# Second block's attention in groups, its scan woven with projections, and a new step order for both blocks' group pipelines

## What is computed

```python
def first_block(...):                       # two layers
    h = _rms(x, ln1[l]) * (1 + sc1) + sh1
    x = x + g1 * _mixing(h, ...)            # top-k attention, stick-breaking, sliding window
    h = _rms(x, ln2[l]) * (1 + sc2) + sh2
    x = x + g2 * _swiglu(h, ...)

def _hybrid_mixer(h, ...):                  # second block, two layers
    proj = h @ w_in
    a_q, a_k, a_v, b_cq, b_ckv, b_kr, c_z, c_xbc, c_dt = split(proj)
    y_a = _diff_attention(a_q, a_k, a_v, lam, subln_g, lambda_init)  # softmax(s1) - lam * softmax(s2), then norm per head
    y_b = _mla(b_cq, b_ckv, b_kr, ...)      # keys and values from a low-rank part
    y_c = _mamba2(c_z, c_xbc, c_dt, ...)    # convolution, decayed scan, gate, group norm
    return concat([y_a, y_b, y_c]) @ w_out

x = x + g_m * _rmsnorm(_hybrid_mixer(h, ...), norm_g[l, 1])
```

## Time and profile before

| | us |
|---|---|
| time, median of 3 runs (lowest, highest) | 3538.05 (3533.71, 3542.37) |
| profiled execution: time, span | 3541.45, 3539.7 |
| PE busy in the span | 3192.5 (90%) |
| DVE busy | 1755.1 (50%) |
| POOL, ACT busy | 832.0 (24%), 705.4 (20%) |
| mean granted clock of PE | 0.913 |

### The profile page before, as it was taken

The page is one execution under the profiler, slowest core; times in us unless marked ns, Lnnn a source line. Parts: engine busy times, 40 slices in busy tenths (PEclk is TensorE's granted clock), DMA queues, the critical chain, the costliest instruction groups (busy, mean ns, idle before and its releaser), DMA issues.

```text
span 3539.7 us, 33580 instructions
## 1 busy us (share of the span) xinstructions
PE 3192.5 (90%) x12312; PEld 2192.8 (62%) x12312; DVE 1755.1 (50%) x3758; ACT 705.4 (20%) x1539; POOL 832.0 (24%) x704
## 2 busy tenths in 40 slices
PE   6877989999987788999979998899997998899996
PEld 3334548888733454888864452488884444378886
DVE  1375337775327543777542265495833347152343
ACT  2233320000113332000012241220202133121110
POOL 0120113444312011344430000144340000124442
PEclk8987799999998788999999978899998978899998
DMA  4111313443211001344221100144420210112221
GB/s 194 57 39 72 143 60 113 173 179 110 90 48 48 24 1 60 130 156 183 106 76 67 71 1 0 72 172 161 179 103 28 76 48 1 48 48 95 77 91 48
DMA packets 38546, 304.89 MB, mean 86 GB/s; under 512 B 4192, under 2 KB 4320, under 8 KB 23920
## 3 DMA queue, kind: packets, MB, share of 16 engines
q1 hardware_dynamic: 38352, 302.68, 23.3%
q0 software_dynamic: 32, 0.07, 0.0%
HBM read 300.63 MB, written 2.10 MB: 86 GB/s over the span
## 4 chain that ended last, share of the span: by engine, by line
PE 78%; DVE 11%; issue 4%; ACT 3%; DMA 2%; POOL 1%; DVEq 0%; SPq 0%; POOLq 0%; ACTq 0%
PE bank L950 43%; PE bank L928 16%; PE bank L1039 4%; PE bank L1294 1%; DVE SPT L2265 1%; PE bank L1147 1%; PE bank L1089 1%; PE bank L1278 1%; PE bank L1076 1%; PE bank L1026 1%; DMA ring<-in_slabs 1%; DVE sel L1931 1%; PE bank L1285 1%; PE bank L1013 1%; DVE m L1930 1%
## 5 line engine op out<-in xcount | busy, mean ns | idle before, releaser
L855 POOL TENSOR_TENSOR SPT<-ring 128x512 f32<-128x512 f32 (+2 forms) x140 | 170.3, 1216 | 1863.3 <-DMA ring<-in_slabs 1244.6
L928 PE MATMUL bank<-hT,ring 128*128 128x512 f32 (+1 forms) x960 | 422.2, 599 | 14.6 <-ACT hT L1604 6.5
L950 PE MATMUL bank<-U,ring 128*128 128x256 f32 x1728 | 406.5, 380 | 0.0
L950 PEld LDWEIGHTS bank<-U,ring 128*128 128x128 f32 x1728 | 326.3, 190 | 43.3
L928 PEld LDWEIGHTS bank<-hT,ring 128*128 128x128 f32 (+1 forms) x960 | 181.3, 190 | 252.1 <-issue 246.1
L1750 DVE SCALAR_TENSOR_TENSOR nw<-sel,c,nw 128x256 f32<-128x256 f32 x504 | 321.8, 638 | 23.2 <-DMA sel<-in_mod_pieces 5.5
L950 PE MATMUL bank<-hT,ring 128*128 128x256 f32 x1216 | 299.8, 397 | 22.4 <-ACT hT L1604 8.6
L950 PE MATMUL bank<-U,SPT 128*128 128x256 f32 x1296 | 311.2, 379 | 0.1
L950 PE MATMUL bank<-hT,SPT 128*128 128x256 f32 x1216 | 287.3, 379 | 0.0
L950 PEld LDWEIGHTS bank<-hT,ring 128*128 128x128 f32 x1216 | 230.3, 195 | 70.9 <-issue 17.2
L950 PEld LDWEIGHTS bank<-U,SPT 128*128 128x128 f32 x1296 | 246.2, 190 | 33.9 <-POOL SPT L860 0.5
(11 more groups left out here) (293 smaller groups left out, 4164.6 us busy)
## 6 DMA issues: line engine op xcount, KB each, us to landing
ring<-in_slabs SPq DMA_DIRECT2D x88, 2048.0 KB, 8.0
sel<-in_mod_pieces SPq DMA_DIRECT2D x144, 512.0 KB, 3.8
ring<-in_slabs SPq DMA_DIRECT2D x8, 1536.0 KB, 7.1
ring<-in_slabs SPq DMA_DIRECT2D x8, 1280.0 KB, 6.0
ring<-in_slabs SPq DMA_DIRECT2D x4, 1664.0 KB, 7.0
ring<-in_slabs SPq DMA_DIRECT2D x2, 1808.0 KB, 7.3
cst<-in_consts SPq DMA_DIRECT2D x1, 2120.0 KB, 24.3
ring<-in_slabs SPq DMA_DIRECT2D x2, 1056.0 KB, 5.3
```

Of the source, the lines that this page charges most:

```text
L855: pool.tensor_tensor(e1, a21, a22, ALU.add).then_inc(*pool_order.up())
L928: mm = pe.matmul(dst, lhs(k), rhs(k), start=(k == 0), stop=(k == n - 1))
L950: mm = pe.matmul(into[j][:, c:c + HALF], lhs[:, k, :], rhs[:, k, :], start=(begin and k == 0), stop=(end and k == kp - 1))
```

## The change

**Slots (both blocks).** A slot is now two chunks, an early one and a late one. Early: `on` of group j-3, then `sc` of group j. Late: `ot` of j-4 (one slot later than before), `pv` of j-2, `tp` of j-1. ACT copies the output of `pv` (and of `bpv`) from its bank as soon as it is there and squares the copy; DVE scales the copy.

**First block.** `pss` stands behind the second part of the next tile instead of behind its fourth.

**Second block.** Attention runs in groups too (`GROUPS2`, 6 of kind `m` with 4 or 2 heads, 12 of kind `d` with 2 heads or 1), `m` first. The division is left to the end (`on`); for `d` a new step `cb` combines both maps after the exponents, and the norm is taken per group from the copy, as in the first block. The order of a layer is: tiles 6 to 9, 4, 5 and the values; a weave of the other projections with the whole scan (called weave 1 here); a weave of tiles 14 to 17 with gate and norm of the scan and the `m` slots (weave 2); a weave of `wo 0` (half of the output projection, over the scan's outputs, 4 k-steps a tile) with the `d` slots (weave 3); then `wo 1`, which DVE adds to the first half. POOL adds up the squares of the output, and one matmul is left of `ys`. The same slabs' contents come in another order and cut; their sum is the same.

```diff
 def group_slots(groups):
-    for j in range(len(groups) + 3):
-        slot = []
+    for j in range(len(groups) + 4):
+        early, late = [], []
+        if 0 <= j - 3 < len(groups):
+            early.append(("on", groups[j - 3]))
         if j < len(groups):
-            slot.append(("sc", groups[j]))
+            early.append(("sc", groups[j]))
+        if 0 <= j - 4 < len(groups):
+            late.append(("ot", groups[j - 4]))
+        if 0 <= j - 2 < len(groups):
+            late.append(("pv", groups[j - 2]))
         if 0 <= j - 1 < len(groups):
-            slot.append(("tp", groups[j - 1]))
-        if 0 <= j - 3 < len(groups):
-            slot.append(("on", groups[j - 3]))
-        if 0 <= j - 2 < len(groups):
-            slot.append(("pv", groups[j - 2]))
-        if 0 <= j - 3 < len(groups):
-            slot.append(("ot", groups[j - 3]))
-        out.append(slot)
-    return [[st] for slot in out for st in slot]
+            late.append(("tp", groups[j - 1]))
+        out += [early, late]
+    return out
...
+        sums = [("pss", TILES1[m - 1])] if 0 <= m - 1 < 16 and TILES1[m - 1] in NORMED else []
+        rope = [("rope", TILES1[m - 2])] if 0 <= m - 2 < 16 and TILES1[m - 2] in ROPED else []
...
-        return [("pj", n, 0), ("pj", n, 1), ("pj", n, 2), ("proj", n)]
+        return [[("pj", n, 0)], [("pj", n, 1)] + sums, [("pj", n, 2)], [("proj", n)] + rope]
...
-UNITS2 = [("d", h, i) for i in range(QT) for h in range(4)] + [("m", h, i) for i in range(QT) for h in range(4)]
+GROUPS2 = [("m", 0, 4, 0), ("m", 0, 4, 1), ("m", 0, 2, 2), ("m", 2, 2, 2), ("m", 0, 2, 3), ("m", 2, 2, 3)]
+NM2 = len(GROUPS2)
+GROUPS2 += [("d", h, 2, i) for i in (0, 1) for h in range(2)] + [("d", h, 1, i) for i in (2, 3) for h in range(4)]
...
+        if 0 <= j - 3 < len(groups):
+            early.append(("on", groups[j - 3]))
+        if 0 <= j - 1 < len(groups) and GROUPS2[groups[j - 1]][0] == "d":
+            early.append(("cb", groups[j - 1]))
+        if j < len(groups):
+            early.append(("sc", groups[j]))
...
+    dense = [c for n in range(4) for c in tile2(n)]
+    dense[8] += [("cqss",)]
+    dense += [[("kvss",), ("kr",)]]
+    dense += [c for n in range(10, 14) for c in tile2(n)]
+    dense += [[("silu", 1)]] + [[("mq", h)] for h in range(4)] + [[("mk", h)] for h in range(4)]
+    dense += [[("mqr", h)] for h in range(4)] + [[("mv", i)] for i in range(QT)]
...
+    o += woven((0.0, 1.0, dense), (0.1, 1.0, scans))
+    slots = group_slots2(range(len(GROUPS2)))
+    keys = [c for n in range(14, 18) for c in tile2(n)]
+    o += woven((0.0, 1.0, keys), (0.0, 0.4, [[("sz",)], [("sn", 0)], [("sn", 1)]]),
+               (0.1, 1.0, [c for slot in slots[:NM2] for c in slot]))
+    o += woven((0.0, 1.0, [[("wo", 0, n)] for n in range(KT)]), (0.0, 1.0, [c for slot in slots[NM2:] for c in slot]))
...
-                        act.activation(osq[g % 2][:, 0:n], src[:, 0:n], ACT.Square).then_inc(*s1["uq"].up())
+                            act.wait_ge(*bk1.ready(l, ("ot", g - 2)))
+                        act.activation(onat[g % 2][:, 0:n], src[:, 0:n], ACT.Copy).then_inc(*freed)
+                        act.wait_ge(*bk1.taken(l, st))
+                        act.activation(osq[g % 2][:, 0:n], onat[g % 2][:, 0:n], ACT.Square).then_inc(*s1["uq"].up())
```

More of the change, by code:

```diff
@@ L335, in order1 @@
     rounds = [[("topk", i, r)] for i in range(1, QT) for r in range(TOPK // 8)]
[L337 to L343, removed]
     def tile(m):
+        sums = [("pss", TILES1[m - 1])] if 0 <= m - 1 < 16 and TILES1[m - 1] in NORMED else []
+        rope = [("rope", TILES1[m - 2])] if 0 <= m - 2 < 16 and TILES1[m - 2] in ROPED else []
+        if m > 15:
+            return [sums + rope]
         n = TILES1[m]
-        return [("pj", n, 0), ("pj", n, 1), ("pj", n, 2), ("proj", n)]
+        return [[("pj", n, 0)], [("pj", n, 1)] + sums, [("pj", n, 2)], [("proj", n)] + rope]
     for m in range(8):
-        o += tile(m) + side(m)
+        o += [st for part in tile(m) for st in part]
         if m == 3:
@@ L358, in order1 @@
     dense = []
[L359 to L362, removed]
+    for m in range(8, 18):
+        dense += tile(m)
     o += woven((0.0, 0.92, dense), (0.24, 1.0, group_slots(range(NC1))),
@@ new lines, in head_of, with group_slots2 @@
+def head_of(group, hh):
+    return group[1] + (hh if group[0] == "m" else 2 * hh)
+def group_slots2(groups):
+    out = []
+    for j in range(len(groups) + 4):
+        early, late = [], []
+        if 0 <= j - 3 < len(groups):
[4 more added lines that the diff above has]
+            early.append(("sc", groups[j]))
+        if 0 <= j - 4 < len(groups) and groups[j - 4] in TURNS2:
+            late.append(("ot", groups[j - 4]))
+        if 0 <= j - 2 < len(groups):
+            late.append(("pv", groups[j - 2]))
+        if 0 <= j - 1 < len(groups):
+            late.append(("tp", groups[j - 1]))
+        out.append([early, late])
+    return out
@@ L465, in order2, with tile2 @@
+def tile2(n):
+    return [[("proj", 3)]] if n == 3 else [[("pj", n, 0)], [("pj", n, 1)], [("pj", n, 2)], [("proj", n)]]
 def order2(l):
     o = [("prep",), ("ns", 0), ("nh", 0)]
[L467 to L470, removed]
@@ new lines, in order2 @@
+    scans = [[("dtt",)]] + [[("xd", i)] for i in range(QT)] + [[("G", g, st)] for g in range(2) for st in range(QT)]
+    scans += [[("da", 0)]]
+    for h in range(10):
+        if h < 7:
+            scans.append([("da", h + 1)])
+        if h < 8:
+            scans += [[("scan", h, st)] for st in range(QT)]
+        if 0 <= h - 1 < 8:
+            scans.append([("y", h - 1)])
+        if 0 <= h - 2 < 8:
+            scans.append([("yo", h - 2)])
+    o += woven((0.0, 1.0, dense), (0.1, 1.0, scans))
@@ new lines, in _ @@
+                        if n == 0 and s == 0:
+                            pe.wait_ge(*s2["hn"].after(l, 7))
+                        elif n == 0:
+                            for g in TURNS2:
+                                pe.wait_ge(*bk2.taken(l, ("ot", g)))
+                        pe.wait_ge(*sl2.ready(l, ("wo", s)))
+                        w4 = ring[:, sl2.slot(l, ("wo", s)), :].rearrange("p (k n) -> p k n", k=4)
+                        right = [U[:, XC + t, :] for t in range(4)] if s == 0 else [hT[:, 0, :], hT[:, 1, :], U[:, MO[0], :],
+                                                                                  U[:, MO[1], :]]
```

627 lines of the change are left out of this document (363 added, 264 removed).

## The result

The changed kernel takes 3439.78 us (median of 4 runs, 3435.46 to 3446.29) where the kernel before took 3535.88 on the same chip (4 runs, 3532.21 to 3542.37): a ratio of 0.9728, 95% interval 0.9706 to 0.9750, 96 us faster. The forecast was 119 us, 3419.

The account below looks back on a forecast made before the run. PE was taken to bound the kernel, busy 90% but at reduced clock and with waits in the mixers. Gains of 70 us (first block) and 49 (second, two layers) made 119, so 3419 us; range 3330 to 3505.

Parts of the forecast that it names:

- The stage bounds: Second block, per layer: weave 1 108 to 135 us, weave 2 50 to 70, weave 3 from 65 to 109.
- its 70 us: First block's mixers: forecast gain, three quarters of 92.9 us of PE waits, with bounds 30 and 110 us.
- The reason given: First block: `pss` earlier, ACT's copy and later `ot` address waits of 34.1 (`rope`), 30.0 (`pv`), 20.7 (`ot`), 8.1 us (`bpv`).
- no wait over 5 us: First block, sign of being right: PE waits at most 5 us in total ahead of `rope`, `pv` and `ot`.
- Weave 1: Second block, remaining projections with the scan: 108 us of PE work plus 10%, 119 us a layer.
- Weave 2: Second block, tiles 14 to 17, gate, norm and `m` slots: 50 us of PE work, 58 us a layer.
- Weave 3: Second block, `wo 0` with `d` slots: 59 us of PE work, rounds of DVE and ACT making it 97 us.
- The wait named: Weave 3: `on` of group j-3 precedes `cb` and `sc` in DVE's queue and waits for ACT behind j-1's exponents.
- POOL's first FFN sums: Second block's end: 10 us of sums move behind the squares' chain, costed at nothing, at most 3 us a layer.
- the slower rival: Second block: PE granted clock 0.55 through all three weaves, 121 us more a layer, 3661 us; chance 0.09.
- The rounds don't hold PE: Rival: ACT and DVE overlap more, weave 3 takes 65 us instead of 97, total 3332 us; chance 0.20.
- dearer clock and chains: Rival: second block's weaves take 135, 68 and 115 us, 44 more a layer, total 3507 us; chance 0.17.

Follow-up runs that it names:

- e1: Changed kernel with the first block's slots, place of `pss` and ACT's copy all put back as before, second block as changed: ratio 0.9964 to the kernel before.
- e4: Changed kernel without ACT's copy in the first block (ACT squares from the bank, DVE's `on` and `bon` read it): ratio 0.9762 to the kernel before.
- e6: Changed kernel with the second block's early chunk in the order `cb`, `sc`, `on` instead of `on`, `cb`, `sc`: ratio 0.9665 to the kernel before.
- e5: Changed kernel with POOL's slab sums of the second block's first two FFN units put ahead of its additions of the squares: ratio 0.9672 to the kernel before.
- e10: Changed kernel with POOL's first two slab sums ahead of the additions, `on` behind `sc`, and `wo 0` tiles inside the slots: ratio 0.9590 to the kernel before.
- e9: Changed kernel with the eight `wo 0` tiles behind the last `d` group instead of between the slots: ratio 0.9781 to the kernel before.
- e11: e10 with weave 1's first 30 projection pieces spread over 0 to 0.8 of it and the last 17 over 0.8 to 1: ratio 0.9623 to the kernel before.

## Why the prediction was right, and where it was off

The total came out near the forecast in part by luck. The first block gave more than its 70 us, and the second, with 49 forecast, gave 24 by the traces and 13 by e1; the two errors cancel in part. The stage bounds of the prediction also don't add up to the bounds it gives for the second block's two layers, 70 lost and 130 gained: with 108, 50 and 65 us for the weaves they make 152 gained, and with 135, 70 and 109 they make 30 lost. The forecast itself doesn't hang on this.

**First block: right, and larger.** Forecast 70 us; 79 by the traces (86 in the mixers), 83 by e1. The mixers are 50.6 and 35.6 us shorter where "some 35" each was said. The reason given was half right: `rope`, `pv` and `bpv` wait no more, but "no wait over 5 us" is wrong for `ot`, 32.5. That the next wait would be for DVE is right, though for its rotation (L2025, 21.3 us, once 12.0) and not for masks: `rope` holds bank 7, and `ot` needs it. The two cures for `pv` overlap (e4).

**Second block: 20.6 us in the first layer, 25 forecast, and by the stretches 21.3 and 10.9 in the two mixers.** By stages, in the first layer: ahead of the weaves 55.5 (56). Weave 1 127.6 (119): the term that was mis-sized, by 9, in PE's work and not in its waits. Weave 2 56.8 (58). Weave 3 94.2 (97), right in sum: its rounds are 6.05 without a tile (6.8 forecast) and 7.9 with one (10.1 at half clock), and 0.80 of the full clock lies between. The wait named, `on` ahead of `cb` and `sc`, is there, and e6 bears it out. The tile in the round was rightly seen to hold up PE's scores, as e6 shows; what I had not seen is that ACT's root stands behind the tile's eviction too. PE's own waits stood more ahead of `pv` (23.6 us, L1372) than of `tp` (9.6). `wo 1` 27.6, the end 9.7 (9.5), 1.8 of it by POOL's work beside DVE's (7.8 in e5).

**The step that failed** is "POOL's first FFN sums ... I cost them at nothing, at most 3 us a layer". They cost 5.9 us a layer, 12 in all (e5), not by coming late but by slowing DVE beside them. The argument looked only at when the sums are needed, and the price stood in the trace of before (1.44 to 1.79 us for 0.75).

**The clock.** The weaves had 0.96, 0.97 and 0.80 and the whole run 0.931, so the slower rival, with 0.55 in all three, is out. Where a round left PE idle the clock was down, 0.80 with PE busy 79% of weave 3, and with fuller rounds (e10) the same weave had 0.89 with PE busy 88%. The rule that the prediction cites from the Trainium skill ("TensorE: Matmul & The Clock Gate", section "A second HAM failure mode: psum-queue depth-cycling"), taken strictly, was that rival; the traces agree with it in kind and not in size. *The rounds don't hold PE* is excluded by e9, whose rounds take 6 us with no tile in them; *dearer clock and chains* is half true of weave 1 alone.

In sum: 119 forecast, less 17 for weave 1 and 12 for POOL, more 8 for weaves 2 and 3 and 9 for the first block, makes 107, against 103 between the spans. What is left is within the spread between the layers, of which I had taken one for both: the same change gained 21.3 us in the first mixer and 10.9 in the second.

## What to carry to other kernels

- In a hand-written order that all engines share, ask for every piece that is woven in what it does on *each* engine. A matmul tile cost a round 1.9 us because its eviction stood ahead of a small step on ACT and the tile itself ahead of PE's next scores; half a slot further on it cost 0.2 to 0.6.
- When work moves to another place in time, ask what runs beside it there, and not only whether it is done in time. Look in the trace for the same pair of engines side by side elsewhere: the price may stand there.
- Two edits that remove one wait each do not sum when both free the same bank; undone one at a time the three parts of the first block's change showed 49 of its 83 us.

## What was not expected of the hardware

DVE operations of 512 columns with both inputs in SBUF took 1.60 to 1.75 us beside POOL's additions and 0.69 to 0.75 without them, and POOL's 1.6 to 1.7 instead of 1.26; a DVE addition with one input in a bank took 0.69 beside the same POOL work. And the clock fell during a stop of PE of 7.3 us, so that the eight matmuls behind it took 4.53 us for 2.37; behind a stop of 3.4 us (e11) they took 4.53 us too.
